# Two feed-forward stages: another order of the last down-projection blocks

## The reference, cut to what matters

```python
# first layer
h = rms_norm(x, g_pre_ffn)
u = causal_depthwise_conv(h @ w_up, conv_w, conv_b)
gate, val = jnp.split(u, 2, axis=-1)
f = (jax.nn.gelu(gate, approximate=True) * val) @ w_down      # 2816 -> 1024
x = x + rms_norm(f, g_post_ffn)
e = p @ w_ple
g = jax.nn.sigmoid(rms_norm(x, g_ple_gate) @ w_ple_gate + b_ple_gate)
x = x + rms_norm(g * e, g_post_ple)
# ... second layer, which ends in
hn = rms_norm_2(h, norm_ffn)
return h + (jax.nn.silu(hn @ w_gate) * (hn @ w_up)) @ w_down   # 2816 -> 1024
```

## Time and profile before

| | |
|---|---|
| median of 3 runs | 951.9 us (949.21 to 952.31) |
| profiled execution | 953.55 us, of which span 951.8 us |
| mean granted TensorE clock | 0.954 of full |
| PE busy | 880.4 us, 92% of the span |
| DVE, ACT, POOL busy | 683.9, 510.7, 322.7 us |
| loads | 137.18 MB, mean 144 GB/s |

### The profile page before, as it was taken

One profiled execution on the slowest core, in us unless ns is written; L12 is line 12 of the kernel. 1 busy time (PEld: TensorE's weight loads), 2 busy tenths in 40 slices (PEclk: granted clock), 3 DMA queues, 4 the chain that ended last, 5 costly groups with the idle time before them and its releaser, 6 DMA issues.

```text
span 951.8 us, 16906 instructions
## 1 busy us (share of the span) xinstructions
PE 880.4 (92%) x6706; PEld 841.3 (88%) x6706; DVE 683.9 (72%) x986; ACT 510.7 (54%) x926; POOL 322.7 (34%) x150
## 2 busy tenths in 40 slices
PE   4997798999999998998999979998997999999998
PEld 3986688999999998887889878987996999999998
DVE  6857642688889897376889989974785576666573
ACT  5467445664555556665763664547544544444441
POOL 3744102222223323533544772332453233223320
PEclk8998588999999998999999999999998999999999
DMA  5734001454556565433445462222453546656541
GB/s 191 281 118 155 23 1 62 139 168 145 165 178 188 174 195 183 152 106 111 164 165 159 131 228 94 90 88 69 133 167 100 159 151 199 197 168 190 178 156 45
DMA packets 54078, 137.18 MB, mean 144 GB/s; under 512 B 6000, under 2 KB 24816, under 8 KB 53872
## 3 DMA queue, kind: packets, MB, share of 16 engines
q1 hardware_dynamic: 54000, 136.11, 44.6%
HBM read 135.03 MB, written 1.05 MB: 143 GB/s over the span
## 4 chain that ended last, share of the span: by engine, by line
PE 70%; DVE 18%; ACT 6%; issue 5%; DMA 1%; SPq 0%; DVEq 0%; ACTq 0%
PE PROD L579 14%; PE PROD L581 13%; PE PROD L580 13%; DVE wlo L1507 3%; DVE RS L1515 3%; PE PROD L641 2%; PE OP L579 2%; PE OP L581 2%; PE OP L580 2%; PE SC L579 2%; PE SC L580 2%; PE SC L581 2%; PE TP L581 2%; PE TP L580 2%; PE TP L579 2%
## 5 line engine op out<-in xcount | busy, mean ns | idle before, releaser
L562 POOL TENSOR_TENSOR wlo<-raw,whi 128x1024 fp32r<-128x1024 f32 x124 | 318.7, 2576 | 605.5 <-ACT whi L1027 605.3
L579 PE MATMUL PROD<-HA,whi 128*128 128x256 f32 x1096 | 317.6, 290 | 14.4 <-DVE HA L1535 6.4
L580 PE MATMUL PROD<-HA,wlo 128*128 128x256 f32 x1096 | 313.4, 286 | 0.0
L581 PE MATMUL PROD<-HA,whi 128*128 128x256 f32 x1096 | 313.2, 286 | 0.0
L1027 ACT ACTIVATE whi<-raw 128x1024 fp32r<-128x1024 f32 x252 | 261.7, 1051 | 50.1 <-PE PROD L581 27.0
L1507 DVE TENSOR_TENSOR wlo<-raw,whi 128x1024 fp32r<-128x1024 f32 x128 | 187.2, 1466 | 99.6 <-ACT whi L1027 99.3
L579 PEld LDWEIGHTS PROD<-HA,whi 128*128 128x128 f32 x1096 | 213.7, 195 | 17.4 <-DVE HA L1535 7.2
L580 PEld LDWEIGHTS PROD<-HA,wlo 128*128 128x128 f32 x1096 | 213.9, 195 | 0.6 <-issue 0.5
L581 PEld LDWEIGHTS PROD<-HA,whi 128*128 128x128 f32 x1096 | 213.7, 195 | 0.0
L1789 DVE SCALAR_TENSOR_TENSOR YC<-Y,CV,YC 128x255 f32<-128x255 f32 x88 | 66.9, 763 | 2.2 <-ACT YC L1221 0.7
L1515 DVE RECIPROCAL RS<-RTT 128x256 f32<-128x256 f32 (+2 forms) x18 | 42.8, 2380 | 20.7 <-ACT RTT L1046 20.7
(11 more groups left out here) (321 smaller groups left out, 1714.8 us busy)
## 6 DMA issues: line engine op xcount, KB each, us to landing
raw<-stream SPq DMA_DIRECT2D x208, 512.0 KB, 3.7
raw<-stream SPq DMA_DIRECT2D x136, 128.0 KB, 2.4
raw<-stream SPq DMA_DIRECT2D x8, 384.0 KB, 3.0
raw<-stream SPq DMA_DIRECT2D x8, 256.0 KB, 3.2
X<-xT SPq DMA_DIRECT2D x2, 512.0 KB, 6.2
E<-memT SPq DMA_DIRECT2D x1, 1024.0 KB, 5.7
out<-X SPq DMA_DIRECT2D x8, 128.0 KB, 2.0
PX<-pT SPq DMA_DIRECT2D x1, 256.0 KB, 3.8
```

The source lines that it names most:

```text
L562: nc.gpsimd.tensor_tensor(wlo[:, n % NSPLIT, :], raw[:, n % NRAW, :], whi[:, n % NSPLIT, :].bitcast(F32), ALU.subtract).then_inc(lo_pool, 1)
L579: nc.tensor.matmul(dst, wh, hi, start=start, stop=False, skip_group_check=True)
L580: nc.tensor.matmul(dst, wl, hi, start=False, stop=False, skip_group_check=True)
L581: last = nc.tensor.matmul(dst, wh, lo, start=False, stop=stop, skip_group_check=True)
```

## The change

The tail's 48 blocks are put in another order, in both networks, in the stream and in PE's program alike: outputs 0 to 3 take chunks 16 to 19 (16 blocks), then outputs 0 to 3 take chunks 20 and 21 (8 blocks), then outputs 4 to 7 take chunks 16 to 21 (24 blocks). The waits stay at the chunks of m = 0.

```diff
+TAIL = [(range(4), range(OUTER, FC - 2)), (range(4), range(FC - 2, FC)), (range(4, 8), range(OUTER, FC))]
+
 def ffn_order(up, down):
...
-    return order + [FIRST[down] + m * FC + k for m in range(8) for k in range(OUTER, FC)]
+    return order + [FIRST[down] + m * FC + k for ms, ks in TAIL for m in ms for k in ks]
...
-                for m in range(8):
-                    for c in range(OUTER, FC):
-                        if m == 0:
-                            pe.wait_ge(a_lo, need_a + c + 1)
-                        partial(m, c)
+                for ms, cs in TAIL:
+                    for m in ms:
+                        for c in cs:
+                            if m == 0:
+                                pe.wait_ge(a_lo, need_a + c + 1)
+                            partial(m, c)
```

## The result

| | before | after |
|---|---|---|
| median | 950.14 us (18 runs) | 943.53 us (18 runs) |
| profiled execution, span | 953.55, 951.8 us | 944.49, 942.7 us |
| mean granted clock, profiled | 0.954 | 0.965 |

The ratio is 0.9921, 95% interval 0.9899 to 0.9942: the kernel became faster by 0.8%, 7.5 us of 950, with an interval from 5.5 to 9.6. The two medians lie 6.6 us apart.

The account below looks back on a forecast made before the run. Matmuls on PE bound the kernel, with serial DVE and ACT work between stages. First tail saves 6.77 us, second network and loads cost 0: 953.55 to 946.8 profiled, median 951.9 - 6.8 = 945.1 us, range 942.9 to 949.0.

Parts of the forecast that it names:

- Where the lost time is: First network's tail: 6.87 us lost, by late chunk 20, PE's wait for chunk 21 (3.92) and low clock (2.65).
- Cover of 17 blocks: First network's tail: chunk 21 wanted at 374.73, ready at 374.60, 0.13 us to spare; 0.1 charged, tail 6.77 us earlier.
- Weights: Weight tiles 93 to 97, tail and ple: all ready in time, smallest slack 1.49 us at tile 97, which moves forward.
- ACT: ACT's outputs, tiles and copies behind the first tail: done about 1.1 us before the root, so no cost.
- Reaches the end: Behind the root: everything hangs on the work before it, so the gain arrives whole; nothing charged for the 2.8 us load wait.
- Second network, loads: Second tail has no wait to win; three more transfers per network, tile 93 in four pieces; both cost 0.
- the last term of the sum: End of the sum: saving taken from the median of three runs, 951.9 - 6.8 = 945.1 us.
- The 946.8 for the profiled execution: Whole profiled span: 953.55 less the first tail's 6.77 us gives 946.8.
- Rival 1: First tail: chunk 21 still late, some 1.2 us wait, perhaps 2.65 of low clock; gain 5.6 or 2.9; chance 0.10.
- Rival 2: Behind the first tail: ACT or loads bind and give time back; gain 4 to 6 us; chance 0.08.
- Rival 3: Both tails: changing accumulator breaks the stream and drops the clock, 7.0 us per network, 959.1 us; chance 0.02.
- Rival 4: Load of tile 93 or 248 late: 2.5 us lost per network or more in one, gain 0 to 3; chance 0.04.

Follow-up runs that it names:

- the filled wait: Kernel before, old order, with 32 unread matmuls put before the first network's wait for chunk 21; median 947.66 against 949.64 us, ratio 0.9976.
- the root was moved forward by 1.43: Changed kernel with the sum of the squares (postffn) moved ahead of ple's first two outputs; medians 941.79 and 941.71 us, ratios to before 0.9897 and 0.99.
- that part alone: Kernel before with the new tail order in the second network only; median 949.34 against 949.64 us, ratio 0.9996.
- chunk by chunk: Against the kernel before, both tails take chunk 16 into all eight outputs, then 17, up to 21; median 948.72 against 949.85 us, ratio 0.9978.

## Where the prediction was right, and the step that failed

- *Where the lost time is:* right. Chunk 20's and chunk 21's wait and the low clock made 6.87 us, and the tail became 6.87 us shorter. The split of it, 4.2 and 2.65, is shown by the filled wait.
- *Cover of 17 blocks:* right, with the margin predicted as 0.13 us and found as 6.11 - 5.98 = 0.13. I had charged 0.1 us for a weight load that comes just late; it came 0.03 us late and cost nothing (tail 17.28). The cover was only just enough: one block less would have left a wait of some 0.2 us, an estimate from 0.36 - 0.13.
- *Weights:* right. No wait on wlo in the tail, tile 97 2.2 us earlier.
- *ACT:* right, 1.07 us to spare against a predicted 1.1; 0.18 left once the root was moved forward by 1.43.
- *Reaches the end:* right as far as it can be followed. From the root to an unchanged small instruction of the next layer (a reciprocal on DVE) at 579.95 before and 567.76 after, the shift is 12.19 us, as it was at the root (12.21). The 3.1 us lost behind that are lost between that instruction and the second feed-forward network. They are not there in every execution of the changed kernel: its second profile has 553.95 us from root to end.
- *Second network, loads:* right, cost 0 (ratio 0.9996 with that part alone).
- *The step that failed is the last term of the sum, the time from which the saving was taken.* "I put the difference on the median: 951.9 - 6.8 = 945.1" takes the median of three runs, 951.9, for the kernel's. Over 18 runs it is 950.14, 1.8 us lower, and 950.14 - 6.8 = 943.3, beside a measured 943.53. So the saving was sized right and the start of the sum was not. The range had the same fault: I had read the spread of three runs (3.1 us) as the spread of the kernel, and it is 9.7 us (946.1 to 955.82). The low end, 942.9, was therefore drawn only 0.6 us below the median that came, and single runs go down to 939.22. The 946.8 for the profiled execution failed in the same way: it was 944.49, because the parts around the tail took 5.34 us less and 3.11 us more.
- *Rival 1:* no rest of the wait stayed. Whether the clock falls behind 1.2 us of idle time, as its price assumed, is not settled: in the tail it did not behind 1.17 and 2.61 us, in one profile each, but elsewhere in these kernels it did behind 1.75 us in 7 of 13 profiles.
- *Rival 2:* not here, but real one step further: chunk by chunk, ACT came to the root at 391.02, 0.85 us after the last matmul of the sum (390.17), where it had always waited for the sum until then, and 4.2 us were given back.
- *Rival 3:* false. By the Trainium skill, TensorE: Matmul & The Clock Gate, in its section on psum-queue depth-cycling, one kernel went round the banks, PE often stood idle for a moment between its groups of matmuls, and the clock swung. Here 48 blocks, each into another accumulator than the one before, leave no idle time in 17.28 us and the clock at 1.00.
- *Rival 4:* no wait on a load for tile 93 or 248 after; 2.9 us at the one place behind, where it was 2.8. The section of the Trainium skill that the prediction names for its 2 us a transfer (DMA: Bandwidth & Descriptors, the anatomy of one DMA) describes transfers issued by GpSimd; here SP issues them, and a piece of 128 KB landed after 2.4 us in the median.

## What to carry to other kernels

Where an engine with an in-order queue waits for the last operands of a stage, look for work already queued behind the wait whose operands are ready, and count the cover in blocks against the time at which the operand is ready: here each block moved was worth 0.36 us until the wait was gone, and more cover would have bought nothing (40 blocks of it gave the same 17.28 us). Then ask who reads what the moved work completes: the same wait covered chunk by chunk cost 4.2 us behind it, since all outputs were complete only at the end and ACT's work on them and on the weights could begin only then. A saving below 1% is read from the stage in the trace, not from the difference of two spans, and a forecast of the time needs more than three runs of the kernel before.

## What the hardware showed beyond that

- One idle stretch of 3.77 us cost 2.65 us more through the clock (1.2 GHz for 5.9 us), in three of four profiles, and 1.44 in the fourth. Filled with matmuls nobody reads it cost none, in one profile. Behind shorter pauses the price varies from execution to execution: a pause of 2.6 us at one place of the second layer was followed by slow matmuls in 4 of 13 profiles, one of 1.75 us at another in 7 of 13.
- On one core the same kernel before ran from 946.1 to 955.82 us in 18 runs. In the first layer's attention the same matmuls (176 and 177 in the records) took 30.69 us at a granted clock of 0.78 in one profile and 27.13 us at 0.91 in another. The tail, which PE fills densely, repeats to 0.03 us; the way up to it differs by 7.2 us between the profiles of the table, the way from the root to the end by 5.4.
